# The first mixer's dilated attention, stepped between the projections of the group that follows

## The reference

```python
proj = jnp.einsum('bsd,de->bse', xn, w_in)
q_a, k_a, v_a, q_r, k_r, v_r, g_r, gate_logits = jnp.split(proj, IN_SPLIT_POINTS, axis=-1)
q_a = apply_rotary(...); k_a = apply_rotary(...)
for g, (window, dilation) in enumerate(((128, 1), (512, 4), (2048, 16))):
    o, l = dilated_window_attention(q_a[:, :, g], k_a[:, :, g], v_a[:, :, g], dilation, window // (2 * dilation))
    outs.append(o); lses.append(l)            # l = max + log(denominator)
mix_w = jax.nn.softmax(jnp.stack(lses, axis=0), axis=0)
y_att = jnp.einsum('gbsh,gbshd->bshd', mix_w, jnp.stack(outs, axis=0))
ret = retention(q_r, k_r, v_r)                # forward and backward decays
merged = g_att * (y_att @ w_attn_branch) + g_ret * ((silu(g_r) * norm(ret)) @ w_ret_branch)
x = x + merged @ w_out                        # then 64 experts, then two layers of the second block
```

## Time and profile before

| | us |
|---|---|
| profiled execution, device time | 3330.52 |
| its span | 3328.7 |
| median of three executions (lowest, highest) | 3331.03 (3318.07, 3335.12) |
| PE busy, share of the span | 2763.0, 83% |
| DVE, ACT, POOL busy | 1159.2, 872.0, 889.4 |
| mean granted TensorE clock | 0.874 |

### The profile page before, as it was taken

How to read it: one execution, slowest core, us unless ns; L and a number is a source line. 1 busy time by engine, 2 the same in 40 slices (tenths; PEclk the granted TensorE clock), 3 DMA queues, 4 the chain that set the end, 5 groups by cost and what they waited for, 6 DMA issues and landing times.

```text
span 3328.7 us, 34893 instructions
## 1 busy us (share of the span) xinstructions
PE 2763.0 (83%) x13364; PEld 1929.8 (58%) x13364; DVE 1159.2 (35%) x1934; ACT 872.0 (26%) x1563; POOL 889.4 (27%) x554
## 2 busy tenths in 40 slices
PE   7898897999747777777777756999999979999998
PEld 5687875778632222222222225768887757688876
DVE  4332234622231111112112125745443346454433
ACT  2223222332201111111111113354332333543323
POOL 3112214544211111111111113223444332234433
PEclk9676978999858888887888877999999989999999
DMA  4101212022349999999999973102232221123221
GB/s 152 43 28 61 76 65 82 26 76 101 127 181 413 409 408 409 406 409 405 408 408 406 404 307 104 51 32 88 84 102 78 100 81 51 51 76 98 80 101 64
DMA packets 134092, 586.89 MB, mean 176 GB/s; under 512 B 15137, under 2 KB 62545, under 8 KB 107985
## 3 DMA queue, kind: packets, MB, share of 16 engines
q1 hardware_dynamic: 117632, 553.64, 42.6%
q10 hardware_dynamic: 9808, 23.15, 1.9%
q0 software_dynamic: 6528, 8.44, 0.7%
HBM read 579.06 MB, written 14.78 MB: 178 GB/s over the span
## 4 chain that ended last, share of the span: by engine, by line
PE 58%; DMA 22%; DVE 8%; ACT 4%; POOL 3%; issue 3%; ACTq 1%; SPq 1%; POOLq 0%; PEldq 0%; PEld 0%; DVEq 0%
PE ps L325 34%; DMA wide<-in_moe_w 20%; PE ps L933 7%; PE ps L1362 4%; PE ps L1346 3%; POOL ring_r L303 2%; PE ps L632 2%; PE ps L588 2%; PE ps L618 1%; PE ps L1338 1%; ACT ring_r L297 1%; DVE xn L359 1%; SPq L1293 1%; PE ps L857 1%; PE ps L410 1%
## 5 line engine op out<-in xcount | busy, mean ns | idle before, releaser
L303 POOL TENSOR_TENSOR ring_r<-ring,ring_r 128x1024 fp32r<-128x1024 f32 (+2 forms) x288 | 704.6, 2479 | 1382.8 <-ACT ring_r L297 1303.8
L1346 PE MATMUL ps<-wide,arena 128*32 128x512 f32 x2048 | 351.5, 820 | 249.0 <-DMA wide<-in_moe_w 248.5
L325 PE MATMUL ps<-xnT_r,ring_r 128*128 128x512 f32 (+1 forms) x1664 | 495.1, 378 | 13.5 <-DVE xn_r L2091 7.2
L325 PE MATMUL ps<-ring_r,xnT_r 128*128 128x512 f32 (+2 forms) x1360 | 441.1, 399 | 35.8 <-POOLq L255 25.0
L325 PEld LDWEIGHTS ps<-xnT_r,ring_r 128*128 128x128 f32 x1664 | 307.7, 190 | 81.4 <-issue 19.6
L325 PE MATMUL ps<-ring_r,arena_r 128*128 128x512 f32 x1392 | 339.0, 401 | 14.3 <-DVE arena_r L2447 10.6
L325 PEld LDWEIGHTS ps<-ring_r,xnT_r 128*128 128x128 f32 (+1 forms) x1360 | 290.5, 225 | 82.7 <-issue 33.2
L1346 PEld LDWEIGHTS ps<-wide,arena 128*32 128x32 f32 x2048 | 67.3, 129 | 451.7 <-DMA wide<-in_moe_w 264.2
L325 PE MATMUL ps<-xn_r,ring_r 128*128 128x512 f32 (+1 forms) x832 | 312.3, 375 | 0.0
L325 PEld LDWEIGHTS ps<-ring_r,arena_r 128*128 128x128 f32 x1392 | 265.3, 193 | 80.6 <-issue 24.9
L297 ACT ACTIVATE ring_r<-ring 128x1024 fp32r<-128x1024 f32 (+2 forms) x288 | 273.7, 1024 | 117.0 <-DMA ring<-in_w_down 60.3
(11 more groups left out here) (311 smaller groups left out, 3447.4 us busy)
## 6 DMA issues: line engine op xcount, KB each, us to landing
wide<-in_moe_w SPq DMA_DIRECT2D x192, 2048.0 KB, 17.1
ring<-in_w_in SPq DMA_DIRECT2D x27, 2048.0 KB, 8.0
ring<-in_w_up SPq DMA_DIRECT2D x22, 2048.0 KB, 8.6
ring<-in_w_down SPq DMA_DIRECT2D x10, 2048.0 KB, 7.7
ring<-in_w_out SPq DMA_DIRECT2D x6, 2048.0 KB, 8.6
ring<-in_w_ret_branch SPq DMA_DIRECT2D x2, 2048.0 KB, 9.7
arena<-expert_rows ACTq DMA_DIRECT2D x4, 1024.0 KB, 8.2
attn_spill<-arena ACTq DMA_DIRECT2D x2, 1056.0 KB, 4.0
```

Source lines behind the costliest of these rows:

```text
L303: nc.gpsimd.tensor_tensor(ring_r[:, q % 2, cols], ring[:, q % 2, cols], ring_r[:, 2 + q % 2, cols].bitcast(F32), ALU.subtract).then_inc(ha ...
L325: ins = nc.tensor.matmul(bank, left, right, start=(start and k == 0), stop=(stop and k == 2))
L1346: res.append(nc.tensor.matmul(ps[g * CAP:(g + 1) * CAP, bank, :], xT[:, c, :], w[:, c, :], start=(c < 4), stop=(c >= KC - 4), tile_positio ...
```

## The change

There are 4 pairs for groups 1 and 2 and 8 for group 0, 16 in all. The joining of the groups has two parts: groups 1 and 2 are merged tile by tile after jobs 3 to 6 of the last stage; group 0, the last, is weighed straight from PSUM when its four chunks of a tile are mixed, and its copy by ACT is gone. Pieces of the diff:

```diff
+            for what, k in M.steps():
+                if what == "chunk":
+                    e, c = k
+                    kind, u, i, _ = M.job(e)
+                    if i == 2 and c % 2:
+                        high_act(a, u + 1, (c // 2,))
...
+                elif what == "return":
+                    a.wait_ge(Z.spilled_out, 16)
+                    a.dma_start(left, spilled[M.leaves - 1].rearrange("(i p) n -> p i n", p=P)).then_inc(Z.spilled_in, 16)
+                elif what == "merge_ask":
+                    a.wait_ge(Z.merge_asked, 1)
+                    nc.scalar.activation(X.merged_e, X.merged_e, ACT.Exp).then_inc(Z.merge_ready, 1)
...
+        def merge_two_dve(v, link, i):
...
+            for g, o in enumerate((X.o1, X.o2)):
+                o3 = by_head(o[:, i, 0:BANK])
+                ins = nc.vector.tensor_tensor(o3, o3, per_head(X.merged_e[:, g, i, :]), ALU.mult)
+            link(ins)
+            nc.vector.tensor_tensor(X.o1[:, i, 0:BANK], X.o1[:, i, 0:BANK], X.o2[:, i, 0:BANK], ALU.add).then_inc(Z.tile_added, 1)
...
+            v.wait_ge(Z.mixed_ready, 4 * (i + 1))
+            o3 = by_head(X.o1[:, i, 0:BANK])
+            nc.vector.tensor_tensor(o3, o3, per_head(e[:, 0, :]), ALU.mult)
+            nc.vector.tensor_tensor(by_head(X.weighed), by_head(ps[:, 6, :]), per_head(e[:, 1, :]), ALU.mult).then_inc(Z.mixed_taken, 1)
+            v.wait_ge(Z.mixed_taken, i + 1)
+            nc.vector.tensor_tensor(X.o1[:, i, 0:BANK], X.o1[:, i, 0:BANK], X.weighed, ALU.add).then_inc(Z.attended, 1)
...
         def retain_act(a):
+            a.dma_start(rows[:, 1], t["ret_gn_w"].partition_broadcast(P)).then_inc(mixer_rows_loaded, 16)
+            a.dma_start(rows[:, 2:4].rearrange("p a n -> p (a n)"), t["b_branch_gate"].partition_broadcast(P)).then_inc(mixer_rows_loaded, 16)
             a.dma_start(R.decay[:, 0:HEADS], t["ret_decay_fwd"].partition_broadcast(P)).then_inc(Z.rows_loaded, 16)
...
-            for g in range(GROUPS):
-                heads_dve(v, g > 0)
+            for g in ORDER:
+                mixer_dve(v, link, mixer_of(g))
                 nxt()
-                attend_dve(v, link, dilated(g))
-                nxt()
-            heads_dve(v, False)
-            combine_dve(v, link)
+            mixer_dve(v, link, mixer_ret())
...
-            for units in ((), (0, 1, 2), (3,), (4, 5), (6,), (7, 8), (9,), (10, 11, 12)):
+            for units in ((0,), (1, 2, 3), (4, 5, 6), (7, 8, 9), (10, 11, 12, 13)):
...
             turn_act(a, xnT_high, KC)
+            high_act(a, 0)
             nxt()
```

More of the change, by code:

```diff
@@ L580, in __init__ @@
                 self.score_bank, self.turn_bank, self.mixed_bank = banks
-        def attend_scores_pe(pe, A, n):
-            i, heads, keys, _ = A.chunks[n]
-            if n >= 2:
-                pe.wait_ge(Z.scores_taken, n - 1)
-            k0, k1 = keys[0][0].start, keys[-1][0].stop
-            for j, hh in enumerate(range(*heads.indices(HEADS))):
-                ins = nc.tensor.matmul(ps[:, A.score_bank[n % 2], j * (k1 - k0):(j + 1) * (k1 - k0)], A.q(hh)[:, i * P:(i + 1) * P],
-                                       A.k(hh)[:, k0:k1], start=True, stop=True)
-            ins.then_inc(Z.scores_ready, 1)
+                self.peaks, self.totals = stats or (res[:, :, BANK:BANK + HEADS], res[:, :, BANK + HEADS:])
         def attend_pair_scores_pe(pe, A, p):
@@ L679, in attend_keep_dve @@
             ins.then_inc(Z.probs_kept, 1)
-        def attend_dve(v, link, A):
-            for n in range(len(A.chunks)):
-                attend_mask_dve(v, link, A, n)
-                if n:
-                    attend_keep_dve(v, A, n - 1)
-            attend_keep_dve(v, A, len(A.chunks) - 1)
         def attend_exp_act(a, A, n):
@@ new lines, in mixer_of @@
+        def mixer_of(g):
+            base = U_ATT + 3 * ORDER.index(g)
+            values = [SHIFTED[i] for i in range(NT + 1)] if g == 0 else [tokens(i, True) for i in range(NT)]
+            jobs = [(kind, base + j, i, tokens(i, g > 0)) for j, kind in enumerate("qk") for i in range(NT)]
+            jobs += [("v", base + 2, i, toks) for i, toks in enumerate(values)]
+            home = X.vr_low if g == 2 else X.va
+            dsts = [home[0:len(range(*toks.indices(S))), i, :] for i, toks in enumerate(values)]
+            q, k = (X.qT, X.kT) if g == 2 else (X.qT_xn, X.kT_xn)
+            earlier = None if g == 1 else dilated(1) if g == 2 else dilated(2)
+            return Mixer(jobs, g > 0, q, k, (DH ** -0.5, 1.0), dsts, earlier, leaves=1 if g == 0 else None)
@@ new lines, in mixer_dve @@
+        def mixer_dve(v, link, M):
+            cos = table("cos_perm" if M.permuted else "cos_nat").rearrange("p (i d) -> p i d", i=NT)
+            sin = table("sin_perm" if M.permuted else "sin_nat").rearrange("p (i d) -> p i d", i=NT)
+            for what, k in M.steps():
+                if what == "chunk" and k[1] == KC - 1:
+                    n = M.entries[k[0]][1]
+                    if n not in M.roped:
+                        continue
+                    m = M.roped.index(n)
+                    v.wait_ge(Z.proj_ready, n + 1)
+                    if m >= 2:
+                        v.wait_ge(Z.turned, m - 1)
+                    rope(ps[:, dense_bank(k[0]), :], X.tmp, X.rot[:, m % 2, :], cos[:, m % NT], sin[:, m % NT], HEADS)
+                    v.wait_ge(Z.taken_dve, m + 1)
+                    nc.vector.tensor_tensor(X.rot[:, m % 2, :], X.rot[:, m % 2, :], X.tmp, ALU.add).then_inc(Z.roped, 1)
+                    v.wait_ge(Z.roped, m + 1)
+                elif what == "merge_ask":
+                    merge_ask_dve(v, link)
+                elif what == "merge":
+                    merge_two_dve(v, link, k)
+                elif what == "scores":
+                    for n in (2 * k, 2 * k + 1):
+                        attend_mask_dve(v, link, M.attention, n)
+                elif what == "turn":
+                    for n in (2 * k, 2 * k + 1):
+                        attend_keep_dve(v, M.attention, n)
+                    if M.merges and k % 2:
+                        last_ask_dve(v, link, k // 2)
+                elif what == "values" and M.merges and k % 2:
+                    last_merge_dve(v, link, k // 2)
@@ new lines, in per_head, with by_head, merge_ask_dve @@
+        def per_head(x):
+            return x[:, :, None].to_broadcast([P, HEADS, DH])
+        def by_head(x):
+            return x.rearrange("p (h d) -> p h d", d=DH)
+        def merge_ask_dve(v, link):
+            tops = [o[:, :, BANK:BANK + HEADS] for o in (X.o1, X.o2)]
+            v.wait_ge(Z.spilled_in, 16)
+            link(nc.vector.tensor_tensor(X.merged_top, tops[0], tops[1], ALU.max))
+            for g in range(2):
+                ins = nc.vector.tensor_tensor(X.merged_e[:, g], tops[g], X.merged_top, ALU.subtract)
+            ins.then_inc(Z.merge_asked, 1)
@@ L2622, in _ @@
             retain_pool(pool)
-            low_pool(pool, U_GATE)
             nxt()
```

392 lines of the change are left out of this document (210 added, 182 removed).

## The result

| | before | changed |
|---|---|---|
| median of four executions (lowest, highest) | 3331.11 us (3318.07, 3335.12) | 3216.97 us (3210.57, 3222.73) |
| ratio, 95% interval | | 0.9663 (0.9631 to 0.9696) |
| profiled execution, its span | 3330.5, 3328.7 | 3216.9, 3215.1 |
| mean granted TensorE clock | 0.874 | 0.902 |

The kernel is 3.4% faster; the forecast was 3225 us. First the windows view of the changed kernel, cut at its stages (us, then busy time and instructions of PE, PEld, DVE, ACT and POOL, PEclk, DMA share, GB/s). The five rows are group 1's projections, the projections of group 2, of group 0 and of the retention, each with the attention of the group before stepped in, and the retention itself. They answer to the earlier trace rows.

What follows compares the result with a forecast made beforehand. The prediction took the attention stages as bound by PE's own matmuls at half clock. Retention's first matmul 110.7 us earlier, less 5 for later decays, gave 3330.5 - 105.7 = 3225 us; range 3198 to 3262.

Steps and rivals of the forecast that it cites:

- start of the first projections: Kernel start: unit 0 rounded before the projections, which open at 35.8 us instead of 29.48, a loss of 6.3 us.
- waits of PE at the steps: Stepped stages: 8 us in all, 3 at a tile's merge and join in the last stage, 5 for two groups.
- retention's first matmul: End of the mixer: it comes at 445.4 instead of 556.1 us, 110.7 us earlier.
- Three signs that the prediction named: Stepped stages of 93 to 96 and 97 to 101 us; retention's first matmul at 437 to 455; decays landing after 8 to 10.
- The clock: Attention steps between projections: run at full clock, 63.2 us in all, with PEclk of 0.93 or more in the stepped stages.
- The rivals at the lower level: Attention steps alone at the lower clock: 3311 us, chance 0.05; stepped stages as a whole: 3564 us, chance 0.03.
- the forecast's own range: Whole kernel: 3200 to 3250 us, from fewer or more waits, stage starts at full clock and the retention's start.
- Stage starts: Openings of stages: three starts that stay at full clock are worth 8 us, counted in the range only.
- Price of a step: Attention of groups 1 and 2 at full clock: 5.7 scores + 4.3 transposes + 6.7 values = 16.7 us each.
- Group 0: Group 0's attention, stepped into the retention's projections: 7.8 + 8.6 scores, 8.6 transposes and 13.4 values, 29.8 us.
- The retention's start: Opening of the retention: decays land 5 us later than the 4.1 before, costing 5 us.
- The step that failed: Retention's start: the decays land late because they stand behind 1.5 MB of gate rows in ACT's queue.

Runs made afterwards that it cites:

- the run beside the experiments: The changed kernel, unedited, measured again in the same rounds as three of the follow-up kernels: 3212.1 us, ratio 0.9646.
- The block: The changed kernel with attention steps of groups 1 and 2 one chunk apart, in the last seven chunks of the next group's stage: 3245.1 us, ratio 0.9752.
- the half distance: The changed kernel with steps 7 chunks apart instead of 14 in the stages of groups 2 and 0: 3219.3 us, ratio 0.9681.
- the last two kernels: Changed kernel with decay loads at the last mixer stage's start: 3209.3 us; also with gate rows loaded last and first rounding beside first projections: 3199.8 us.

## Why the prediction came out, and where it did not

Start to start, in us, with the forecast's own terms:

| | forecast | measured | |
|---|---|---|---|
| start of the first projections | 35.8 | 34.7 | -1.1 |
| group 1's projections | 78.7 | 76.6 | -2.1 |
| group 2's, with group 1's attention | 94.4 | 91.5 | -2.9 |
| group 0's, with group 2's | 98.4 | 93.2 | -5.2 |
| the retention's, with group 0's | 130.1 | 136.0 | +5.9 |
| waits of PE at the steps | 8 | in the rows above | -8 |
| retention's first matmul | 445.4 | 432.0 | -13.4 |
| retention stage, beyond 74.5 | 5 | 9.1 | +4.1 |
| all behind it, beyond before | 0 | 1.4 | +1.4 |
| profiled execution, less before's | -105.7 | -113.6 | -7.9 |

The end came out closer than the parts. The mixer was 13.4 us faster than forecast, and the retention and what follows 5.5 us slower; that they offset each other is luck. Three signs that the prediction named were missed: the first two stepped stages are under their 93 and 97 us, the retention's first matmul came at 432.0 and not at 437 to 455, and the decays landed 11.5 us after the opening, not 8 to 10.

**The clock.** Right, and shown twice: by the 0.99 to 1.00 of the stepped stages (in the last of them 0.95 to 0.99 over all the traces), and by the extra wide matmuls in the kernel before. The rivals at the lower level fell; they needed PEclk under 0.85.

**Stage starts.** The forecast's own range had 8 us for starts that stay at full clock, and its value none. The first 48 matmuls of group 1's, group 2's, group 0's and the retention's stage take 13.2, 12.0, 11.4 and, scaled up from 45 of them (10.7), 11.4 us, against 14.25, 13.25, 14.2 (29.48 to 43.66, beside POOL) and 13.74 before: 1.0, 1.2, 2.8 and 2.3 less. This is 1.0 of the -2.1. With the cheaper steps (the next point, 1.9 us in each of two stages) and less the waits of 0.6, it is 2.5 of the -2.9 and 4.1 of the -5.2. In the stepped stages it belonged in the value: it follows from the same step as the clock. Group 0's part comes from the rounding that was moved: its stage used to begin beside POOL, and the forecast took its 80.2 us over as they were.

**Price of a step.** 4.2 us a pair was counted, 3.70 came. The scores were too dear: 0.089 each came from the duration of eight, where sixteen now take 1.09 from start to start, 0.068 each. So were the transposes, 0.11 from start to start and not 0.135.

**Group 0.** Under-sized: all 128 value matmuls were priced at 0.105. Half of them stand in tiles that mix 64 and 128 rows of keys, and four pairs cost 2.91, 2.91, 2.71 and 2.71 instead of 1.73, together 4.3 us. The chain of before shows the same at the lower clock level, a chunk of mixed heights and one of 128 rows alone, and it was not looked at per chunk:

```profile
124.34 2.47 PE ps L632 x8
...
145.86 1.60 PE ps L632 x8
```

One step at a lower clock (1.37 and 2.00 against 0.88 and 1.06) adds 1.4 in this run; in the run beside the experiments that step was at 1.06. With PE's idle time of 3.5, less 2.3 for the earlier start and 1.6 for the cheaper transposes, this makes 5.3 of the +5.9.

**Waits.** 8 us counted, 4.6 found (0.56, 0.55 and 3.5: each window's length less PE's busy time and the boundary), none of it behind the exponentials. The block and the half distance show why: a pair's chain on DVE and ACT is 6.5 to 6.7 us, and 14 chunks are twice as much cover as it needs. The one wait of 1.8 is for a rotary tile (L782) that stood behind the join of a tile, as foreseen. What stretched that chain are DVE's instructions that POOL held up, 6.7 us for three of them: without POOL's reads the wait was gone.

**The retention's start.** The direction was right, the size was not: 7.3 us later for the decays, against the 5 counted. The step that failed is the reason given for it. The queue order was blamed, and putting the decays first gave 3 of the 7.4 us back. Beside them ran unit 14. It is issued when PE is through with the last projections, as before; but then 7.7 us passed until the retention opened, and the unit landed as the decays were issued (548.42 and 7.9 us more, against 556.08). Now it is issued 1.4 us before the opening (430.55 against 431.98) and takes 12.2 us. The Trainium skill's rule of turns between queues (DMA: Bandwidth & Descriptors, Queues, rings and completion order) agrees with that: by it a load that is first in its own queue is still held by the other queue's, 8.1 us here against 3.8 before. That the two queues' share is the whole of the rest was not tried; unit 14 was not delayed.

## What to carry to other kernels

Short matmuls back to back can hold TensorE at its lower clock without a wait between them (0.52 to 0.54 here). Put them between wide ones, and count on the starts of the following stages getting cheaper too; test it beforehand with dummy wide matmuls between the short ones. When a stage is removed, list the loads that it spread in time: a load of 4 KB on the critical path belongs into the stage before, not at the head of a crowded moment. Price every shape of a moved matmul from its own row, the mixed tile heights above all.

## What was not expected of the hardware

- Nine 128x512 matmuls after each attention chunk raise the granted clock of these stages from 0.52 to 0.54 to 0.86 to 0.92 and cost nothing (ratio 1.0009); three gave 0.66 to 0.78, with changes of level within a stage, and a spread of 46 us between executions.
- A VectorE instruction of 8 columns takes 2.37 us when GpSimd's subtraction runs, 0.17 us when GpSimd writes zeros.
- Value matmuls that alternate 64 and 128 rows cost 0.17 to 0.18 us each, those of 128 rows alone 0.11.
- A load of 4 KB, broadcast to 128 partitions, landed after 2.5 and 3.8 us in the kernel before, and after 7.2 to 10.1 us beside a unit of 2 MB, wherever it stood in its own queue. In the last two kernels it took 7.3 to 8.2 us too, at the start of the last mixer stage, beside the 1 MB of the spill and another unit.
